# Two levels of a block's scores in one slot, and a broadcast in another PSUM bank: an encoder layer on one Trainium2 core

## What is computed

```python
def step(state, inp):
    qb, kb, vb, gb = inp
    b = jnp.cumsum(gb, axis=2)
    diff = b[:, :, :, None, :] - b[:, :, None, :, :]
    decay = jnp.exp(jnp.where(causal_in_chunk, diff, -jnp.inf))
    scores = jnp.einsum("bhtd,bhsd,bhtsd->bhts", qb, kb, decay)
    o = (jnp.einsum("bhts,bhsv->bhtv", scores, vb)
         + jnp.einsum("bhtd,bhdv->bhtv", qb * jnp.exp(b), state))
...
o_fwd = chunked_gated_recurrence(qh, k_f, vh, logf_f)
o_bwd = jnp.flip(chunked_gated_recurrence(jnp.flip(qh, 1), jnp.flip(k_b, 1),
                                          jnp.flip(vh, 1), jnp.flip(logf_b, 1)), 1)
gate = jax.nn.silu(g.reshape(bsz, seq, HGRN_HEADS, HGRN_DV).astype(jnp.float32))
y_rec = (rms_norm(o_fwd + o_bwd, out_norm) * gate).astype(h.dtype).reshape(bsz, seq, V_WIDTH)
```

## Time and profile before

| | us |
|---|---|
| median of 3 runs | 2586.88 |
| lowest, highest | 2583.71, 2588.74 |
| the profiled execution | 2589.4 |
| its span in the trace | 2587.6 |

### The profile page before, as it was taken

One profiled execution on the slowest core, in us unless ns is written; L12 is line 12 of the kernel. 1 busy time (PEld: TensorE's weight loads), 2 busy tenths in 40 slices (PEclk: granted clock), 3 DMA queues, 4 the chain that ended last, 5 costly groups with the idle time before them and its releaser, 6 DMA issues.

```text
span 2587.6 us, 45418 instructions
## 1 busy us (share of the span) xinstructions
PE 2528.4 (98%) x18650; PEld 2286.9 (88%) x18650; DVE 1649.2 (64%) x1927; ACT 1369.9 (53%) x1559; POOL 263.5 (10%) x238
## 2 busy tenths in 40 slices
PE   7999999999996999999999999999999999999998
PEld 6787877788886999999999999999999999999997
DVE  6455555435377766667666676766767666676767
ACT  6434353424545555655555555555555555555556
POOL 3102020101111010110101001010110101101010
PEclk9999999999997999999999999999999999999999
DMA  4001010126327676766767677676776767667677
GB/s 157 29 19 54 2 54 2 57 100 216 139 107 273 241 251 226 258 238 231 265 215 269 221 260 251 227 251 228 250 248 230 251 227 251 239 239 255 223 257 276
DMA packets 62486, 503.73 MB, mean 195 GB/s; under 512 B 7568, under 2 KB 8080, under 8 KB 37808
## 3 DMA queue, kind: packets, MB, share of 16 engines
q1 hardware_dynamic: 46224, 448.88, 48.0%
q0 software_dynamic: 16160, 53.38, 6.9%
HBM read 465.07 MB, written 37.22 MB: 194 GB/s over the span
## 4 chain that ended last, share of the span: by engine, by line
PE 67%; DVE 1%; ACT 1%; DMA 0%; issue 0%; POOL 0%; DVEq 0%; POOLq 0%; ACTq 0%
PE up_banks_b L1978 15%; PE up_banks_a L1978 15%; PE up_banks_b L1981 6%; PE up_banks_a L1981 6%; PE up_banks_b L1998 2%; PE up_banks_b L1996 2%; PE up_banks_b L1997 2%; PE up_banks_b L1995 2%; PE up_banks_a L1999 2%; PE up_banks_b L1999 2%; PE up_banks_a L1996 2%; PE up_banks_a L1998 2%; PE up_banks_a L1995 2%; PE up_banks_a L1997 2%; PE up_banks_a L1976 1%; PE up_banks_b L1976 1%
## 5 line engine op out<-in xcount | busy, mean ns | idle before, releaser
L1805 DVE TENSOR_TENSOR big_lo<-ew_raw,big_hi 128x4096 fp32r<-128x4096 f32 x192 | 849.6, 4425 | 419.9 <-ACT big_hi L1645 419.8
L1645 ACT CAST big_hi<-ew_raw 128x4096 fp32r<-128x4096 f32 x192 | 697.3, 3632 | 506.8 <-PE up_banks_a L1978 223.7
L1978 PE MATMUL up_banks_b<-x_parts,big_hi 128*128 128x384 f32 x2048 | 582.9, 356 | 0.0
L1978 PE MATMUL up_banks_a<-x_parts,big_hi 128*128 128x384 f32 x2016 | 573.8, 356 | 0.0
L1981 PE MATMUL up_banks_b<-x_parts,big_lo 128*128 128x192 f32 x1792 | 449.0, 251 | 0.0
L1981 PE MATMUL up_banks_a<-x_parts,big_lo 128*128 128x192 f32 x1764 | 442.0, 251 | 0.0
L1978 PEld LDWEIGHTS up_banks_b<-x_parts,big_hi 128*128 128x128 f32 x2048 | 371.0, 189 | 0.0
L1978 PEld LDWEIGHTS up_banks_a<-x_parts,big_hi 128*128 128x128 f32 x2016 | 365.1, 189 | 0.6
L1981 PEld LDWEIGHTS up_banks_b<-x_parts,big_lo 128*128 128x128 f32 x1792 | 341.4, 191 | 0.0
L1981 PEld LDWEIGHTS up_banks_a<-x_parts,big_lo 128*128 128x128 f32 x1764 | 336.1, 191 | 0.6
L64 PE MATMUL bank<-big_hi,w_hi 128*128 128x512 f32 x576 | 236.9, 411 | 0.0
(11 more groups left out here) (308 smaller groups left out, 4093.2 us busy)
## 6 DMA issues: line engine op xcount, KB each, us to landing
ew_raw<-in_expert_weights SPq DMA_DIRECT2D x192, 2048.0 KB, 7.7
w_raw<-in_w_heads SPq DMA_DIRECT2D x48, 256.0 KB, 2.8
x_in<-in_x SPq DMA_DIRECT2D x12, 512.0 KB, 4.5
x_d<-in_x POOLq DMA_DIRECT2D x12, 512.0 KB, 3.9
residual<-x_d POOLq DMA_DIRECT2D x12, 512.0 KB, 2.9
ffn_in<-h_and_xT_d POOLq DMA_DIRECT2D x12, 512.0 KB, 2.9
ew_raw<-residual SPq DMA_DIRECT2D x12, 512.0 KB, 5.0
tab<-in_tables POOLq DMA_DIRECT2D x10, 512.0 KB, 7.5
```

What stands on the lines that cost most here:

```text
L1645: nc.scalar.copy(w_hi[:, c % RING], raw[:, c % RAW]).then_inc(hi_done, 1)
L1805: nc.vector.tensor_tensor(w_lo[:, c % RING], raw[:, c % RAW], w_hi[:, c % RING].bitcast(F32), ALU.subtract).then_inc(lo_done, 1)
L1978: last = nc.tensor.matmul(out[:, 0:2 * CAP], hi, x[:, k], start=n == 0, stop=n == KT - 1, skip_group_check=True)
```

## The change

Four edits, all in the heads phase. A tuple `LEVELS_AT` says which levels a slot has: slot 0 has levels 0 and 1, slot s for 1 to 6 has level s + 1, slot 7 none. On ScalarE the gather for level 1 is put ahead of the wait for level 0 and of its copy to `near`. And the broadcast for the second block of a head goes to a score bank like that for the third. The turns of banks 2 and 3 shift with it. No instruction is added or taken away on any engine.

```diff
+        LEVELS_AT = ((0, 1),) + tuple((level,) for level in range(2, LEVELS + 1)) + ((),)
...
             for s in range(8):
                 if n < NN:
-                    timeline.append(("level", n, s))
+                    timeline += [("level", n, level) for level in LEVELS_AT[s]]
...
-            elif ev[0] in ("kt", "u") and ev[2] == 1 or ev[0] == "bc" and ev[2] == 2:
+            elif ev[0] in ("kt", "u") and ev[2] == 1 or ev[0] == "bc" and ev[2] >= 1:
...
                     elif kind == "level" and ev[2] == 0:
                         n = ev[1]
+                        gather_keys(n, 0)
                         filled(act, ev)
                         i = fill_of[ev][0]
                         if n >= 1:
                             was_read(act, ("level", n - 1, NEAR))
                         nc.scalar.copy(near[:], near_view[i]).then_inc(bank_read[i], 1)
-                        gather_keys(n, 0)
```

## The result

| | before | changed |
|---|---|---|
| median, us | 2583.71 (7 runs, 2582.48 to 2588.74) | 2593.99 (7 runs, 2591.40 to 2596.04) |
| the profiled execution | 2589.4 | 2593.14 |
| its span | 2587.6 | 2591.3 |

The changed kernel is slower: ratio 1.0034, 95% interval 1.0024 to 1.0043, which is 8.8 us with 6.2 to 11.1; the two medians stand 10.3 apart, inside the interval. The forecast was 2596.6 with a range of 2590 to 2604.

What follows compares the result with a forecast made beforehand. TensorE, busy 98% of the span, was taken as the bound, so its pauses are paid in full. Pause +14.6, isolated level −2.4 and broadcast −2.5 give +9.7 us on a median of 2586.9: 2596.6, range 2590 to 2604.

Steps and rivals of the forecast that it cites:

- The pause: Slot 0: TensorE waits at level 1 for keys ScalarE gathers, 1.20 or 1.24 us a block, 14.6 us lost.
- The isolated level: Level 1 beside level 0 instead of between two half projections saves 0.20 us a block, 2.4 us in all.
- The broadcast: Second block's broadcast, in a score bank, no longer waits for the copy of V: 3 × 0.84 = 2.5 us saved.
- What is moved: Levels 2 to 7 go up a slot; later copies, squares and gates are covered, so it costs nothing.
- the nearest cover: Block 3, slot 5: squares delayed by eight score copies still end 0.9 us before the sums needing them.
- The sum: All terms: +14.6 − 2.4 − 2.5 = +9.7 us, median 2596.6, 0.37% slower.
- (a): Rival: clock falls in the new pauses, 20 us more (2617) in every block, 2603 in a third; chance 0.09.
- (b): Rival: keys are there in time at level 1, not slower, 2582.0 with no pause; chance 0.06.
- (c): Rival: a middling pause at level 1 of about 0.8 us, +4.7 us, 2591.6; chance 0.15.
- (d): Rival: another wait replaces the broadcast's, 2.5 us back, 2599.1; included in the forecast's 0.70.

Runs made afterwards that it cites:

- early gather: Changed kernel with ScalarE's gather for level 1 put ahead of its two k_tok copies: 2585.04 us, ratio 1.0002 to the kernel before.
- u between: Changed kernel with the previous block's two u products put between level 0 and level 1 in slot 0: 2583.09 us, ratio 0.9993 to the kernel before.
- the ladder alone: Changed kernel with the second block's broadcast left in bank 4, run twice: 2598.46 and 2598.71 us, ratios 1.0048 and 1.0052 to the kernel before.
- broadcast alone: Kernel before with only the second block's broadcast moved to a score bank: 2581.73 us, ratio 0.9986.
- before, second: The unchanged kernel before, profiled once more: 2584.21 us, span 2582.4.
- swapped and early: Early gather plus the two key transposes swapped and block 0's gather ahead of V's copy: 2580.10 us, ratio 0.9977 to the kernel before.
- late gather: Changed kernel with the gather for level 1 put back behind the near copy: 2596.93 us, ratio 1.0041 to the kernel before.

## Why the prediction was right

- **The pause, +14.6 us.** Right, by mechanism and size: twelve waits for keys with 14.6 us (15.5 less the 0.9 of before). The single blocks differ a little from the working (1.17 in block 4 for 1.24, 1.29 in block 6 for 1.20), since idle time is counted from level 0's modelled end and the gather started up to 0.15 late. That the sum came out to the tenth has luck in it: four blocks were 0.09 above the working and the others 0.03 to 0.07 below it. The runs with the early gather and with u between show the cause, each by removing another part of it.
- **The isolated level, −2.4 us.** Nearly right: the ladder alone saved 2.0 beside its waits, and level 1 costs 0.49 beside level 0 where 0.40 to 0.48 was taken, against 0.66 before. Gaps before a level that are put down to issue fell from 92 to 81, eleven and not twelve.
- **The broadcast, −2.5 us.** The mechanism right, the size low: 3.2 in the ladder, 3.5 alone. The term took the idle time for the cost of the wait; the wait cost 0.2 to 0.3 us more each time. That the last head has no such wait was read from a list that ends at 560, while its broadcasts stand at 570 to 572; it is right all the same, since TensorE's waits from 560 to 580 show none for them.
- **What is moved, nothing.** Right: no wait at the sums of squares, at intra or at the transposes; the nearest cover held with 1.2 us where 0.9 was reckoned.
- **The sum.** +9.7 forecast, +9.4 in the phase by the profiles, +8.8 by the ratio. The errors of the two savings, 0.4 too much and 0.7 too little, partly cancel. The forecast time was 2.6 above the median because it started from three runs with a median of 2586.88, while seven gave 2583.71.
- **Rivals.** (a) the clock kept 1.00 in the phase with all its pauses. The Trainium skill (TensorE: Matmul & The Clock Gate, A second HAM failure mode: psum-queue depth-cycling; the forecast names another section) tells of a kernel in which frequent small pauses between groups of products made the clock swing; the trace doesn't show this for twelve pauses of 1.2 us in 500 us. (b) and (c) fell with the waits of 1.2 to 1.3. (d) fell with the run of the broadcast alone.

## What to carry to other kernels

When two steps of a chain are put side by side on the bottleneck engine, count what is left on it between the trigger and the use, and on the helping engine everything that its order puts ahead of the helper's step: here 0.40 us of cover against two copies and a gather. Here the remedy was not to undo the move: the idle time of the helping engine just ahead (0.75 us here) had room for the step. Then check the ring of banks, since a step that is put in between changes which steps share a bank; here that was another 0.35 us a block. The gain is to be weighed too: the ladder without its pause was worth some 1.4 to 2 us of 2584, less than the broadcast's bank with its single edit.

## What was not expected of the hardware

Nearly the same pause at the change of phase had two outcomes for the clock. In the 4 us from the end of the pause on TensorE was busy throughout, and the mean clock was:

| execution | pause, us | clock behind it |
|---|---|---|
| before, first | 2.70 | 0.57 |
| before, second | 2.49 | 1.00 |
| broadcast alone | 2.42 | 1.00 |
| u between | 2.50 | 0.64 |
| early gather | 2.53 | 1.00 |
| swapped and early | 2.40 | 0.58 |
| late gather | 2.38 | 0.57 |

The same kernel is in it both ways, and the shortest pause fell while the one of 2.53 didn't: in these runs the length of the pause alone doesn't decide. The pauses of 1.17 to 1.46 us inside the heads phase never lowered the mean clock of its windows.

And a removed wait with 0.84 us of idle time gave back 1.1 to 1.2 us, as the rows of the broadcast show.
